# The opening of a two-block transformer kernel: first modulation block by halves of features, interleaved with the contraction halves of the first three dense rounds

## The reference

```python
cond = jax.nn.silu(c)                                   # c: (1, 1024)
mod = cond @ w_ada[l] + b_ada[l]                        # w_ada: (1024, 6144), 24 MB
sh1, sc1, g1, sh2, sc2, g2 = jnp.split(mod[:, None, :], 6, axis=-1)
h = rms_norm(x, norm1_gain[l]) * (1.0 + sc1) + sh1      # x: (1, 256, 1024)
proj = h @ w_in[l]                                      # w_in: (1024, 4864)
hq, hf, hi, hg, aq, ak, av, gate_h, gate_a = jnp.split(proj, split_pts, axis=-1)
...                                                     # attention, a recurrent branch, gates
x = x + g1 * (merged @ w_out[l])
h2 = rms_norm(x, norm2_gain[l]) * (1.0 + sc2) + sh2
x = x + g2 * moe_ffn(h2, ...)                           # 32 experts, 384 MB of weights
```

## Time and profile before

| | |
|---|---|
| time, median of 3 runs | 1562.98 us |
| the 3 runs | 1560.12, 1562.98, 1564.08 us |
| span of the profiled execution (first to last instruction) | 1556.6 us |
| what lies around the span, against the median | 6.4 us |
| TensorE (PE) busy | 1447.0 us, 93% of the span |
| VectorE (DVE) busy | 602.6 us |
| ScalarE (ACT) busy | 342.8 us |
| DMA | 594.63 MB, mean 382 GB/s |

### The profile page before, as it was taken

One profiled execution on the slowest core, in us unless ns is written; L12 is line 12 of the kernel. 1 busy time (PEld: TensorE's weight loads), 2 busy tenths in 40 slices (PEclk: granted clock), 3 DMA queues, 4 the chain that ended last, 5 costly groups with the idle time before them and its releaser, 6 DMA issues.

```text
span 1556.6 us, 20902 instructions
## 1 busy us (share of the span) xinstructions
PE 1447.0 (93%) x8692; PEld 754.9 (48%) x8692; DVE 602.6 (39%) x920; ACT 342.8 (22%) x395; POOL 22.7 (1%) x36
## 2 busy tenths in 40 slices
PE   5999999999999999999998989999989999998677
PEld 2878985333333333333332333333338999854343
DVE  4686683232223232231321321323247687522111
ACT  4564332010101010110100100101033384321110
POOL 1100100000000000000000000000000000000000
PEclk9999999999999999999999999999999999999889
DMA  9986589999999999999999999999996446999998
GB/s 383 372 324 264 197 351 395 430 428 428 429 427 427 428 429 427 429 427 429 428 428 429 426 427 429 429 427 428 429 403 229 163 163 261 362 386 423 422 422 343
DMA packets 76385, 594.63 MB, mean 382 GB/s; under 512 B 5499, under 2 KB 6753, under 8 KB 36901
## 3 DMA queue, kind: packets, MB, share of 16 engines
q1 hardware_dynamic: 74000, 588.25, 91.5%
q0 software_dynamic: 1792, 4.86, 0.9%
q10 hardware_dynamic: 532, 0.64, 0.1%
HBM read 592.66 MB, written 1.06 MB: 381 GB/s over the span
## 4 chain that ended last, share of the span: by engine, by line
PE 60%; DMA 34%; DVE 3%; issue 1%; SPq 1%; ACT 1%; POOL 0%; DVEq 0%; ACTq 0%
PE PS L563 54%; DMA ring<-in_w_up 26%; DMA ring<-in_w_up_e 6%; PE PS L743 3%; DMA arena<-in_w_in 2%; DMA ring<-in_w_down_e 1%; PE PS L763 1%; PE PS L1528 1%; DVE ring_r L361 1%; DVE arena L853 1%; PE PS L679 1%; SPq L1093 1%; ACT ring_r L356 0%; POOL arena_r L1119 0%; PE PS L1605 0%
## 5 line engine op out<-in xcount | busy, mean ns | idle before, releaser
L563 PE MATMUL PS<-ring,arena 128*64 128x512 f32 x3020 | 671.2, 597 | 41.0 <-DMA ring<-in_w_up 28.7
L563 PEld LDWEIGHTS PS<-ring,arena 128*64 128x64 f32 x3020 | 212.3, 137 | 462.1 <-issue 400.1
L563 PE MATMUL PS<-arena 128*128 128x128 f32 (+12 forms) x1240 | 228.7, 441 | 2.9 <-DVE arena L2109 0.9
L841 DVE TENSOR_SCALAR arena<-PS 128x512 f32<-128x512 f32 x32 | 22.1, 692 | 482.6 <-PE PS L563 482.6
L542 ACT ACTIVATE arena<-arena 128x512 f32<-128x512 f32 x32 | 20.2, 630 | 698.5 <-DVE arena L841 698.5
L563 PE MATMUL PS<-ring_r 128*128 128x256 f32 (+1 forms) x576 | 171.6, 305 | 0.1
L563 PEld LDWEIGHTS PS<-arena 64*128 64x128 f32 (+6 forms) x1240 | 108.6, 164 | 120.4 <-issue 114.9
L563 PE MATMUL PS<-hT_r,ring_r 128*128 128x256 f32 x800 | 151.7, 286 | 0.3 <-DVE ring_r L361 0.3
L361 DVE TENSOR_TENSOR ring_r<-ring,ring_r 128x2048 fp32r<-128x2048 f32 x51 | 116.4, 2291 | 37.2 <-ACT ring_r L356 36.1
L563 PEld LDWEIGHTS PS<-hT_r,ring_r 128*128 128x128 f32 x800 | 127.8, 193 | 2.3 <-issue 1.4
L356 ACT ACTIVATE ring_r<-ring 128x2048 fp32r<-128x2048 f32 x51 | 97.2, 1912 | 104.6 <-PE PS L563 99.2
(11 more groups left out here) (382 smaller groups left out, 965.2 us busy)
## 6 DMA issues: line engine op xcount, KB each, us to landing
ring<-in_w_up SPq DMA_DIRECT2D x128, 2048.0 KB, 20.7
ring<-in_w_down SPq DMA_DIRECT2D x59, 2048.0 KB, 18.6
ring<-in_w_in SPq DMA_DIRECT2D x17, 2048.0 KB, 11.2
ring<-in_w_gate_e SPq DMA_DIRECT2D x14, 2048.0 KB, 19.3
ring<-in_w_down_e SPq DMA_DIRECT2D x13, 2048.0 KB, 20.1
ring<-in_w_up_e SPq DMA_DIRECT2D x13, 2048.0 KB, 19.0
ring<-in_w_ada SPq DMA_DIRECT2D x12, 2048.0 KB, 16.1
ring<-in_w_out SPq DMA_DIRECT2D x4, 2048.0 KB, 7.7
```

The costliest lines, as they stand in the source:

```text
L563: return nc.tensor.matmul(o, w, m, start=first, stop=last)
L841: V.tensor_scalar(glu.rearrange("p (kk b q) -> p kk b q", kk=4, b=2), hu[:, :, :, :, 0], 7.0, None, ALU.min)\
```

## The change

- Block 0 of the modulation is loaded and computed by halves of features: first the columns 0 to 511 of the shift and of the scale, for all 1024 rows, then the columns 512 to 1023. `mod_load(m)` and `mod_products(m)` take the place of `unit_load` and `ada` for m = 0 to 3; m = 0 and 1 are the two contraction halves of the first half of features, m = 2 and 3 those of the second. Each m is loaded by four DMAs of 0.5 MB in runs of 2 KB.
- The two contraction parities land in different column groups, and `mod_columns(half)` adds and transposes them in one product with `pair_sum`.
- Rounds 0, 1 and 2 are computed by contraction halves: `opening_tokens` and `opening_cols` for the blocks k = 0 to 3 of all three, then for k = 4 to 7. Round 1 becomes two pieces of 1024 columns a partition. All the first halves are loaded ahead of the second half of the modulation. `mod_products(2)` and `(3)` run between the columns of round 2's first half.
- Piece 3 (second half of round 0) also has its lower part made by POOL.
- h: ACT, not DVE, multiplies x by the reciprocal root (L1266); the transposed rows are first copied from PSUM to SBUF (`hN`, half by ACT L1274, half by DVE L2079), and the modulation reads them there, by halves: four blocks on ACT (L1282), four on DVE (L2096), then the difference (L2099).
- The norm's squares and root come ahead of silu(c) on ACT and DVE. ACT issues six DMAs for the bias where it issued four.
- Round 3's slot, and those of the following modulation units, are assigned anew; `early_load(4, ...)` moves from behind round 5 to behind round 7. Nine of the small constant loads on POOL become two early ones and seven behind round 0.

```diff
-PRE_UNITS = [(("ada", 0, 0), 0), (("ada", 0, 1), 1), (("ada", 0, 2), 2), (("ada", 0, 3), 3), (("in", 0), 9), (("in", 1), 0),
-             (("ada", 1, 0), 1), (("in", 2), 2), (("ada", 1, 1), 3), (("in", 3), 9), (("ada", 1, 2), 1), (("in", 4), 0),
-             (("ada", 1, 3), 3), (("in", 5), 2), (("ada", 2, 0), 1), (("in", 6), 3), (("ada", 2, 1), 0), (("in", 7), 1),
+PRE_UNITS = [(("ada", 0, 0), 0), (("ada", 0, 1), 3), (("in", 0), 9), (("in", 1), 11), (("in", 2), 10), (("ada", 0, 2), 2),
+             (("ada", 0, 3), 1), (("in", 3), 0), (("ada", 1, 0), 3), (("ada", 1, 1), 2), (("in", 4), 1), (("ada", 1, 2), 3),
+             (("ada", 1, 3), 9), (("in", 5), 0), (("ada", 2, 0), 2), (("in", 6), 3), (("ada", 2, 1), 9), (("in", 7), 1),
...
+            for half in range(2):
+                mod_load(2 * half)
+                mod_load(2 * half + 1)
+                for r in range(OPENING):
+                    opening_half(r, half)
+            sp.dma_start(consts[:, NFIRST:], t["consts"][:, NFIRST:]).then_inc(S("consts"), 16)
...
+            pool_lower(0)
             nc.gpsimd.memset(at(A1MAP, "reset"), 1.0).then_inc(S("reset"), 1)
...
+            pool_lower(OPENING)
+            pool.wait_ge(S("big_done"), 1)
...
+            act.wait_ge(S("h_transposed"), 2)
+            A(*hN_half(0), ACT.Copy).then_inc(S("hN"), 1)
+            split_upper(act, 0)
+
+            def upper_half(half):
+
+                act.wait_ge(S("hN"), 2)
+                act.wait_ge(S("modT"), half + 1)
+                for k in range(4 * half, 4 * half + 4):
+                    last = A(hT_up[:, k, :], hN[:, k, :], ACT.Identity, scale=sm("scaleT")[:, k:k + 1],
+                             bias=sm("shiftT")[:, k:k + 1]).then_inc(S("hT_A"), 1)
...
+            def modulated(half):
+
+                v.wait_ge(S("ada_done"), 2 * half + 2)
+                sig(TV(mod_sums[:, half, :], mod_sums[:, half, :], PS[:, 7, :], ALU.add), "modrow")
+                v.wait_ge(S("rowsT"), half + 3)
...
+                v.wait_ge(S("hN"), 2)
+                for k in range(4 * half, 4 * half + 4):
+                    last = TS(h_full[:, k, :], hN[:, k, :], sm("scaleT")[:, k:k + 1], sm("shiftT")[:, k:k + 1], ALU.mult, ALU.add)
+                L(last)
+                v.wait_ge(S("hT_A"), 4 * half + 4)
+                sig(TV(hT_low[:, c, :], h_full[:, c, :], hT_up[:, c, :], ALU.subtract), "hT_lower")
...
+            modulated(0)
+            for n in range(1, OPENING):
+                split_lower(v, n)
...
+            def opening_tokens(r, half):
+
...
+                pe.wait_ge(S("w_upper"), n + 1)
+                for m, (a, w) in enumerate(((xu, wu), (xl, wu), (xu, wl))):
+                    if m == 1:
+                        pe.wait_ge(S("hT_lower"), half + 1)
+                    if m == 2:
+                        wait(pe, lower_ready(n))
...
+            mod_products(0)
             pe.wait_ge(S("posf"), 1)
...
             transpose_h(pe, "n1")
...
+            mod_products(1)
+            keep_warm_short(4, 6)
+            mod_columns(0)
+            keep_warm_short(8, 6)
+            opening_tokens(0, 0)
+            pe.wait_ge(S("hN"), 2)
+            opening_tokens(1, 0)
+            opening_cols(2, 0, lambda c: mod_products(2 + c))
+            mod_columns(1)
+            opening_tokens(0, 1)
+            opening_tokens(1, 1)
+            opening_cols(2, 1)
             ada(4)
...
+            split_cols(3)
             ada(5)
             ada(6)
-            split_cols(3)
```

More of the change, by code:

```diff
@@ L192, in program, with mod_landed, landings @@
         SLOT_OF = [slot_of(u) for u in range(MOE2 + NSLOT)]
+        MOD_SLOTS = [SLOT_OF[u] for u, d in enumerate(PRE) if d[:2] == ("ada", 0)]
+        def mod_landed(m, c):
+            if m % 2 and c:
+                return S(f"loaded{MOD_SLOTS[m]}"), 32
+            return S(f"loaded{MOD_SLOTS[m - m % 2]}"), 96
+        def landings(s, before):
+            return SLOT_OF[:before].count(s) + 5 * MOD_SLOTS[0::2].count(s) + MOD_SLOTS[1::2].count(s)
         def slot_used(u):
@@ L424, in quad_loaded @@
             s_ = quad_slot(q, i)
[L425 removed]
+            n = (s_ in HALVED) + landings(s_, MOE2) + sum(1 for p in range(q + 1) if s_ in (QUAD0, QUAD1, LATER)[min(p, 2)])
             if register is None:
@@ L1531, in ada, with mod_products @@
                 last.then_inc(S("ada_done"), 1)
+            def mod_products(m):
+                w = mod_view(m)
+                for c in range(2):
+                    wait(pe, mod_landed(m, c))
+                    for s_ in range(2):
+                        for kk in range(2):
+                            k, j = 4 * (m % 2) + 2 * c + kk, 2 * s_ + kk
+                            last = nc.tensor.matmul(PS[32 * j:32 * j + 32, 7, :], sm("cond32")[:, 32 * k:32 * k + 32],
+                                                    w[:, 2 * c + kk, s_, :], start=m % 2 == 0 and c == 0,
+                                                    stop=m % 2 == 1 and c == 1, tile_position=(0, 32 * j))
+                last.then_inc(S("ada_done"), 1)
@@ new lines, in opening_cols @@
+            def opening_cols(r, half, between=None):
+                n, o = half * OPENING + r, PS[:, banks(r), :].rearrange("p b (c t) -> p (b c) t", c=2)
+                ks = slice(4 * half, 4 * half + 4)
+                wu, wl, xu, xl = upper(n), PIECES[n][3], hT_up[:, ks, :], hT_low[:, ks, :]
+                wait(pe, lower_ready(n))
+                for c in range(4):
+                    cs = slice(c * P, (c + 1) * P)
+                    for k in range(4):
+                        for m, (a, w) in enumerate(((xu, wl), (xl, wu), (xu, wu))):
+                            last = mm(o[:, c, :], w[:, k, cs], a[:, k, :],
+                                      half == 0 and c % 2 == 0 and k == 0 and m == 0,
+                                      half == 1 and c % 2 == 1 and k == 3 and m == 2)
+                    if c == 3:
+                        last.then_inc(S("big_done" if half else "half_done"), 1)
+                    elif between and c < 2:
+                        between(c)
```

381 lines of the change are left out of this document (189 added, 192 removed).

## The result

The changed kernel takes 1564.96 us (median of 20 runs, 1558.30 to 1569.96). The kernel before, run beside it, takes 1558.49 (20 runs). One of those 20 took 2448.58; without it their median is 1558.33. The ratio is 1.0037, with a 95% interval of 1.0027 to 1.0046: **5.8 us slower** (the medians alone are 6.5 apart). The forecast of 1565.0 met the time almost exactly, but by luck. It was a forecast of +2.0 on a kernel whose three first runs had a median of 1562.98, and with twenty runs that median is 4.5 lower. So the difference is the fairer test. It came out 3.8 larger than predicted, just past the 0.3% from which I call a kernel slower. To that case I had given 0.25.

A forecast was written before the change was run, and what follows sets the result against it. PE was taken to set the pace up to the experts, handing on any opening gain or loss. Profiled span 1556.6 + 2.0 = 1558.6, with 6.4 around it 1565.0 us; range 1560.0 to 1570.0.

The forecast's parts named there:

- The start and the first half of the modulation: Opening on PE: first product at 14.9 us, 2.1 later than before; first dense product at 25.9, where it was 32.95.
- POOL holds DVE: Round 0: POOL's 4.55 us subtraction holds DVE's blocks of h, so PE waits for `hT_low` from 28.0 to 31.35.
- Rival 1: POOL and DVE don't collide, or only the difference is held: stall 0.8 to 2.3 us, total 1562.5 to 1563.9; chance 0.22.
- The clock: PE's clock behind the `hT_low` stall: forecast to stay up, as it did through an earlier wait of 3.05 us.
- rival 3: The clock falls in the `hT_low` stall: at most 4.2 us more, total 1568 to 1569; chance 0.2.
- The second hand-over: Behind `mod_columns(1)`, before round 0's second half: 1.05 us of new idle time on PE, to 49.75.
- Round 5's load: Round 5's weights: slot free at 79.1 us, landed by 86.3, when ACT comes to them at about 86.
- The sum: Opening on PE: start +2.1, data waits -3.5, clock +0.6, hand-overs and holds the rest: +1.7 at 81 us, +2.0 at 99.6.
- The 6.4: Whole kernel: 6.4 us around the profiled span, added to the forecast span of 1558.6 to give 1565.0.
- What lies behind round 6: After the opening, up to the experts: PE sets the pace, so the opening's +2.0 us is handed on unchanged.

The follow-up runs named there:

- e4: The change with a semaphore for each modulation load and `mod_columns(1)` ahead of the last part of round 2's first half: ratio 1.0014, median 1560.93 us.
- e1: The change with the lower part of piece 0 made by DVE instead of POOL: ratio 1.0012 to the kernel before, median 1561.08 us.
- e9: The changed kernel run once more, nothing edited: ratio 1.0049 to the kernel before, median 1566.37 us.
- e5: The change with round 5's weights in round 2's slot and the early expert load behind round 8: ratio 1.0022, median 1561.98 us.
- e8: The kernel before, with only round 0's product order taken from the change (`hT_low` second, lower weights third): ratio 1.0016, median 1561.71 us.
- e7: The change with the edits of e4 and e5, and DVE making piece 0's lower part as in e1: ratio 0.9991, median 1557.74 us.
- e3: The change with twelve products of the identity in the stall ahead of the product with `hT_low`: ratio 1.0017, median 1562.02 us.
- e2: The change with the lower-weights product ahead of the `hT_low` product in the first two rounds' halves: ratio 1.0010, median 1560.69 us.
- e6: The change with the edits of e2, e4 and e5, and POOL's two memsets ahead of its subtraction: ratio 0.9983, median 1555.12 us.

## Why the prediction was right or wrong

- **The start and the first half of the modulation** were right: first product 14.86 for 14.9, first dense product 25.75 for 25.9. The data bounded it as said: the wait is one for `w_ada`. e4 shows that the shared semaphore, which I had taken as given, was 0.9 of it.
- **POOL holds DVE** was right, and the step on which most hung. The wait was 3.23 where 3.3 stood, with two errors in it that cancel: POOL began 1.2 earlier than I had placed it (23.19 for 24.4), and its memset, which I had left out, holds DVE for 0.9 more. The rule of the Trainium skill (SBUF — State Buffer, "SBUF: two separate sides") agrees with both: it names any GpSimd operation as the other side of the lock, and makes an exception only for a VectorE operation with two SBUF inputs against a GpSimd operation that does not read SBUF. My own argument for the hold, that DVE reads SBUF at twice the rate of PSUM, set 1024 columns against 256; like for like it is 0.29 against 0.475.
- **Rival 1**, no collision, fell with e1 (1.38 beside 5.28). Its 0.22 was too much, as the earlier trace rows already had a subtraction that ended behind POOL's.
- **The clock** is the step that failed. The forecast had it stay up, by the wait of 3.05 ahead of 26.46; I gave rival 3 only 0.2. It fell, and in e9, e4, e5 and e8 again, and in e7 behind a later stall. I had priced it at up to 4.2 for one fall. There were two, and together they cost 2.2 up to `ada(4)` (e3): half speed was over before the second group ended. The forecast had some of this in hand, 0.3 from a stall that ended earlier and 0.5 in the second half. What is left: second half at 51.16 for 49.75, `ada(4)` at 66.90 for 65.4, transposes at 84.47 for 82.9, scan at 79.42 for 77.9, each 1.4 to 1.6 late.
- **The second hand-over**: 1.18 for 1.05. But I had counted it as a cost of its own only and missed that the clock falls a second time behind it.
- **Round 5's load "in time"** was wrong. Issued at 81.00 rather than 79.1, it landed at 90.39, not 86.3: 9.4 us from issue to landing, where I had 7.2. It did not queue behind other loads: around its start the DMA was far from full, with 193 GB/s in 80 to 82 and 265 in 82 to 84, where I had put 390. By the packets in the trace its own run from 82.02 to 89.84, from 88.06 on beside those of the next unit. What it cost is at least the 0.4 of e5, whose load still came late; that the order of e2 leaves a wait of 3.27 on it and a lag of 0.3 speaks for a small cost.
- **The sum.** At round 6: forecast +2.0, 1.5 late at `ada(4)` by the clock, load 0.4 make +3.9, against +4.2 in this execution and +5.1 in e9's. The first is accounted for to within 0.3. The 0.9 between two executions of the same kernel is not.
- **The time was met by luck.** 1565.0 is 1556.6 + 2.0 + 6.4. The 6.4 set the span of one execution against the median of three others. Every execution of which both are known has 1.7 to 1.9 us between its span and its time. So 1556.6 stood for 1558.4, close to the 1558.49 of twenty runs, and the sum should have read 1560.4. The 4.6 too much there and the 4.5 too little in the difference (+2.0 for 6.5 by the medians) cancelled.
- **What lies behind round 6** the forecast had at nothing, as "handed on". The profiled execution of the change ends 11.3 behind that of before: 4.2 at round 6, 5.6 at 159, 10.1 at 261, but 7.9 at 1345, where the second block's experts begin, and 11.0 at 1365. That of e9 ends 9.8 behind: 5.1, 6.4, 6.4, 7.6, 9.0. In both, two falls of the clock add to the opening, near 150 (1.4 and 1.3) and near 1350 (3.1 and 1.4), and neither adds anything in e5, which has the same opening and is 3 us faster by its median. These executions are on the slow side of their kernel (1569.67 and 1568.21, with medians of 1564.96 and 1566.37).
- **What stays open** is why these later falls come, and how often in executions without a profile. The change's runs spread wider than those of before (1558.3 to 1570.0), and the slower ones have the lower clock: 0.987 in the run of 1558.30, 0.977 in that of 1569.67. That fits more or fewer such falls; no run tells what decides their number.

## What to carry to other kernels

Before moving work of VectorE from PSUM to SBUF, look where GpSimd runs: beside it a cheap operation with one source lasts as long as GpSimd does, memsets included. Put the product that needs the held result last, behind one whose operands are there (e2, e6); that mends the stall wherever the collision falls, while moving the work off GpSimd mends it only in one place (e7). And price a stall of TensorE of about 3 us at more than itself: here some 2 us came on top, part of it behind a later, shorter gap. Last, don't add to a profiled span what another execution's time exceeds it by.

## What the runs showed of the hardware that I had not expected

- A memset on POOL, which only writes, holds DVE's `tensor_scalar` from SBUF to SBUF just as its subtraction does: DVE goes on at 28.71 behind a memset that ends at 28.64, and in e6, without it, right behind the subtraction. It does not hold DVE's difference with two sources in SBUF. In the kernel before, such a memset (35.66 to 36.61) lies over L2010, which ends at 37.86. That is 2.15 behind the end of POOL's subtraction (35.71), and such a difference takes 2.29 by itself, so it ran beside the memset.

```profile
35.66 0.95 POOL L1120 MEMSET arena<- 128x1024 f32 x1
```

- The clock fell to the lower level (groups of 2.91 to 3.50 us instead of 2.12) behind stalls of 3.23, 2.83 and 2.72 us that came some 2 us after dense work had begun (in e7: after eight products behind a stretch of 2-column ones), and not in the wait of 3.05 ahead of 26.46. The length of the stall alone does not tell. What the Trainium skill says (TensorE: Matmul & The Clock Gate, "What's actually happening"), that idle time brings the gated clock back, agrees with the direction. But the fall itself came 0.3 to 1.2 us after TensorE had gone on (31.4 for 31.07 in the change, 32.0 for 30.79 in e4), and near 1350 it came with no wait in the rows at all.
- Behind the second gap, of 1.18 us in each, the clock fell in the three executions in which it had fallen at the first (the change twice, and e5), and stayed up in the three in which it hadn't (e1, e2, e3). Whether the first fall causes the second was not tried by itself; the gap also ends 1.1 to 2.7 us earlier in those three (50.08, 48.65 and 50.06, against 51.16 to 51.42), and its place in time may be what counts.
